# A third slot holds a block of the second chunk's mix; the first twenty gathers go round six slots

## The reference

```python
q = (xc @ w_q).reshape(PEER_CHUNK, PEER_HEADS, 2, PEER_HALF)
sc = jnp.einsum('chid,hikd->chik', q, sub_keys)          # 2 x 128 scores for each head
...                                                       # the best 16 of 16 x 16 sums: 16 experts for each head
u_e = jnp.take(u_tab, expert, axis=0)
v_e = jnp.take(v_tab, expert, axis=0)
act = jax.nn.gelu(jnp.einsum('chkd,cd->chk', u_e, xc))
return jnp.einsum('chk,chkd->cd', gate * act, v_e)
```

## Time and profile before

| | us |
|---|---|
| median of 3 executions | 1703.78 (1702.72 to 1705.15) |
| the profiled execution | 1706.91 |
| its span, first to last instruction | 1704.9 |
| busy in the span: TensorE | 1555.9 (91%) |
| VectorE | 1213.1 (71%) |
| ScalarE | 611.8 (36%) |
| GpSimd | 592.6 (35%) |
| moved by DMA | 675.14 MB, mean 396 GB/s |

### The profile page before, as it was taken

How to read it: one execution, slowest core, us unless ns; L and a number is a source line. 1 busy time by engine, 2 the same in 40 slices (tenths; PEclk the granted TensorE clock), 3 DMA queues, 4 the chain that set the end, 5 groups by cost and what they waited for, 6 DMA issues and landing times.

```text
span 1704.9 us, 19518 instructions
## 1 busy us (share of the span) xinstructions
PE 1555.9 (91%) x6554; PEld 938.1 (55%) x6554; DVE 1213.1 (71%) x3361; ACT 611.8 (36%) x1459; POOL 592.6 (35%) x527
## 2 busy tenths in 40 slices
PE   9999899899999999988998889989999999777776
PEld 8877775447467777544645446535656554232232
DVE  7821899985887659997555677995666777667665
ACT  4142432553344233364332242354433223222222
POOL 0000353442334333343333432343333544443331
PEclk9999999999999999999999999999999999999999
DMA  9655999999999999999999999999999999999996
GB/s 383 254 197 203 372 396 421 404 410 421 421 420 414 416 421 420 420 420 422 421 421 421 421 421 422 388 412 384 421 415 418 421 421 422 421 421 421 422 421 271
DMA packets 93859, 675.14 MB, mean 396 GB/s; under 512 B 10408, under 2 KB 10688, under 8 KB 12224
## 3 DMA queue, kind: packets, MB, share of 16 engines
q0 software_dynamic: 73728, 536.90, 76.2%
q1 hardware_dynamic: 20032, 137.00, 19.8%
HBM read 672.81 MB, written 1.05 MB: 395 GB/s over the span
## 4 chain that ended last, share of the span: by engine, by line
PE 34%; DMA 33%; DVE 13%; ACT 4%; issue 2%; POOL 0%; DVEq 0%; POOLq 0%; ACTq 0%
DMA slots<-expert_rows,expert 33%; PE bank L960 18%; PE bank L466 6%; DVE slots L1961 5%; PE bank L649 3%; PE bank L948 2%; PE bank L945 2%; ACT diag L1460 1%; DVE sg L1499 1%; ACT L1473 1%; DVE htok L1776 1%; DVE coef L1499 1%; DVE x L1499 0%; DVE cands L1942 0%; PE bank L737 0%
## 5 line engine op out<-in xcount | busy, mean ns | idle before, releaser
L960 PE MATMUL bank<-slots,diag 128*128 128x512 f32 x1916 | 907.0, 609 | 127.6 <-ACT diag L1460 123.9
L1088 POOL DMA_INDIRECT slots<-expert_rows,expert x512 | 590.7, 1154 | 1087.3 <-PE bank L960 856.7
L1961 DVE CUSTOM_DVE_ANT_0 slots<-slots,htok 128x1024 f32<-128x1024 f32 x512 | 625.2, 1222 | 266.9 <-DMA slots<-expert_rows,expert 263.0
L960 PEld LDWEIGHTS bank<-slots,diag 128*128 128x128 f32 x1916 | 347.5, 193 | 537.5 <-issue 316.8
L1473 ACT ACTIVATE gel<-dot 128x2 f32<-128x2 f32 (+1 forms) x258 | 52.5, 203 | 597.9 <-DVE dot L1961 589.3
L1460 ACT ACTIVATE diag<-ident,coef 128x128 f32<-128x128 f32 x479 | 168.5, 395 | 204.1 <-DVE coef L1499 195.1
L466 PEld LDWEIGHTS bank<-hT,ring 128*128 128x128 f32 x1488 | 181.6, 194 | 40.9 <-issue 38.4
L466 PE MATMUL bank<-hT,ring 128*128 128x128 f32 x1488 | 182.6, 277 | 1.8 <-DMA ring<-w_blocks 1.0
L1499 DVE SCALAR_TENSOR_TENSOR coef<-gel,ginv,gexp 128x2 f32<-128x2 f32 (+1 forms) x258 | 54.7, 212 | 93.8 <-ACT gel L1473 91.9
L1473 ACT ACT_TABLE_LOAD x67 | 86.0, 1283 | 1.2
L1499 DVE SCALAR_TENSOR_TENSOR sg<-pad,prm,sg 128x128 f32<-128x128 f32 x240 | 71.4, 342 | 0.0
(11 more groups left out here) (353 smaller groups left out, 1544.7 us busy)
## 6 DMA issues: line engine op xcount, KB each, us to landing
ring<-w_blocks SPq DMA_DIRECT2D x90, 1024.0 KB
slots<-w_blocks SPq DMA_DIRECT2D x24, 1024.0 KB, 10.8
slots<-expert_rows,expert POOLq DMA_INDIRECT x512
kept<-w_blocks SPq DMA_DIRECT2D x4, 1024.0 KB, 12.2
keys<-w_blocks SPq DMA_DIRECT2D x2, 1024.0 KB
kv<-w_blocks SPq DMA_DIRECT2D x2, 1024.0 KB, 13.8
prm<-small SPq DMA_DIRECT2D x2, 768.0 KB
x<-x_rows SPq DMA_DIRECT2D x2, 512.0 KB, 11.0
```

Of the source, the lines that this page charges most:

```text
L960: last = mm(bank[h][:, :], diag[:, i % DIAGS, :], slots[:, SLOT[n], D + h * 512:D + (h + 1) * 512], start=m == 0, stop=n == end)
L1088: nc.gpsimd.indirect_dma_start(slots[:, s, :], None, experts_d, bass.IndirectOffsetOnAxis(ap=idx[q % 2][:, k:k + 1], axis=0),).then_inc(ar ...
L1961: v.tensor_tensor_reduce(out=slots[:, s, 0:D], in0=slots[:, s, 0:D], in1=htok[:, ph % 2, :], scale=1.0, scalar=0.0, op0=ALU.mult, op1=ALU.add,
```

## The change

Block 4 of step 1's mix, q1, is held in slot 6 from the opening on, as the third held block, and so it is moved ahead of step 1's other blocks in SP's order and goes no more through the ring. `wq` 3 of step 0, which lay in slot 6, goes to slot 2, where `mo` 0 lay. The first twenty gathers go round six slots (0, 1, 3, 4, 5, 2) instead of seven, and from gather 20 on the gathers go round all nine in another rotation.

```diff
-HELD = {2: 8, 3: 7}
-SLOT = [n % 7 for n in range(20)] + [(6, 8, 0, 1, 7, 2, 3, 4, 5)[n % 9] for n in range(NG - 20)]
+HELD = {2: 8, 3: 7, 4: 6}
+SLOT = [(0, 1, 3, 4, 5, 2)[n % 6] for n in range(20)] + [(0, 1, 3, 8, 4, 7, 5, 6, 2)[n % 9] for n in range(20, NG)]
...
             if ci == 1 and what < 2:
                 return WIDE + STAY + what
+            if ci == 0 and h == 3:
+                return place_of_slot(2)
             if ci == 1 and what in HELD:
                 return place_of_slot(HELD[what])
```

## The result

The changed kernel takes 1708.7 us (median of 17 executions, 1705.89 to 1711.3) against 1703.68 us for the kernel before (17 executions, 1702.72 to 1708.03). The ratio is 1.0026, with a 95% interval of 1.0020 to 1.0033: 4.4 us slower, 3.4 to 5.6 (the two medians are 5.0 us apart). The forecast was 1703.5 us, within 0.2% of no change, and the range ended at 1707.8. It was wrong.

What follows compares the result with a forecast made beforehand. The prediction took DMA's bytes as the bound, with engines late in 228 to 247 us. It summed -2.4 and +2.1 to -0.3 us, forecasting 1703.5 us against the median 1703.78, range 1699.8 to 1707.8.

Steps and rivals of the forecast that it cites:

- What bounds the kernel: Whole kernel: DMA is nearly always full, so bytes moved early count unless it later lacks free slots.
- The new wait in the opening: Opening: `wq` 3 waits for `mo` 0's read; seven loads issue in a row from 155.9 us, none wanted early.
- The load that moves: Opening: q1 goes into idle DMA time, giving a 1.0 MB lead at 186 us, -2.4 us (bounds 0 and -2.5).
- Six slots instead of seven: First twenty gathers: each waits for the add six before; cost +2.1 us, the middle of 0 and +4.1.
- The lead starts the dots earlier: 186 to 228 us: dots wait for DMA, so a lead starts VectorE's full stretch earlier, by up to 2.4 us.
- Gather 25 behind q1's read: Around 247 us: gather 25 cannot go before q1's slot is read, at 246.66 us.
- The fixed round: Rival, gathers of 190 to 233 us: issue-to-data time does not shrink, 3.52 us a gather, 1708.4 us; chance 0.16.
- The lead is kept: Rival, first gathers: a slot's round need take only 16 us, DMA never runs dry, -2.4 us, 1701.4 us; chance 0.20.

Runs made afterwards that it cites:

- wq3_late: Kernel before with only `wq` 3 moved to slot 2, so it and the loads behind it wait for `mo` 0; two held blocks, seven slots: +0.05%.
- before2: The kernel before, unedited, profiled a second time: 1702.80 us.
- eight_slots: Kernel before with one held block instead of two (the gate goes through the ring) and eight slots for the first 24 gathers: +0.15%, 2.6 us slower.
- nine_slots: Kernel before with no held block and nine slots from the first gather: +0.29%, 5.0 us slower.
- six_early: Kernel before with its opening and two held blocks kept, but six slots for the first twenty gathers: +0.35%, 6.0 us slower.
- six_then_seven: Kernel before with six slots for gathers 0 to 11, then seven to gather 19, then nine: +0.12%, 2.0 us slower.
- seven_then_six: Kernel before with seven slots for gathers 0 to 6, then six for gathers 7 to 19, then nine: +0.15%, 2.6 us slower.

## Why the prediction was wrong, point by point

- *What bounds the kernel*: right. DMA's bytes decide, and most of a loss before 250 us is carried to the end.
- *The new wait in the opening*: right, seven loads in a row. The wait costs nothing in wq3_late, where six loads stand in the row.
- *The load that moves, -2.4 us*: the lead was there, and DMA moved 422 GB/s from 158 to 186 us. At 186 us it was 0.9 MB against before2, and 1.7 against the profile from which 1.0 was forecast. That a held block is worth 2.5 us where slots suffice fits eight_slots and nine_slots.
- *Six slots instead of seven, +2.1 us with ends 0 and +4.1*: this step failed. Alone the six slots cost 6.0 us (3.9 to 8.0), about three times the 2.1 that was forecast; the interval just reaches the upper end. The prediction held the issued bytes against the moved ones only at 228 and 237 us, and took DMA for full up to 228 because it was full there before. Its sign, more than 400 GB/s in 206 to 228 us, failed at 381; DMA was short from 198 us on. In the changed kernel's profile the count at 198 us, just behind the longest pause of the gathers, gives 17.8 MB issued and 17.5 moved: all but dry. With the prediction's own figures (11.8 MB by 186 us and 421 GB/s behind it) 16.9 would have been moved and 0.9 left, so that the count at 198 would have warned and not have given the size. It leant besides on 376 GB/s at seven slots as its nearest row, a figure that the second profile does not repeat.
- *The lead starts the dots earlier*: wrong in its sign. Dot 5 came at 201.11 us and dot 11 at 219.01, in before2 at 200.40 and 215.29. That DMA, where slots limit its supply, only comes to its end sooner by being ahead is argued; no run shows it by itself.
- *Gather 25 behind q1's read*: it waited for that read as forecast, at 250.15 instead of some 247, but it is not the cause: six_early, in which q1 is not held, has the whole loss.
- *The fixed round* (chance 0.16, 1708.4 us) comes nearest in time: +7.0 for the slots and -2.4 for the lead, where the runs give +6.0 for the slots and an unsettled part of the lead. In part that is luck, for its mechanism was that the time from issue to data does not shrink, and it does shrink: from issue to dot, gathers 14 to 20 took 11.4 us in the mean in before2, 10.0 in the changed kernel and 8.5 in six_early. It had priced 3.52 us a gather against 3.02; the runs have a smaller difference, 3.06 in six_early and 2.85 in the changed kernel's profile against 2.64 in before2. Its sign, a DMA share below 0.95, came in 206 to 214 us (0.94) and already from 198 (0.90), though not in 214 to 228 (1.01), and over the whole of 206 to 228 the share is 0.98. The split of the loss between six_then_seven (6 gathers that wait for the sixth before them) and seven_then_six (8) fits an even price for each gather, within the error. Of the Trainium skill's rule on gaps and too few buffers ("Perfetto Trace Analysis", section "Optimization Strategy") the prediction said that the trace agrees only in 228 to 247 us; with six slots it agrees from 198 us on.
- *The lead is kept*: its estimate was 16 us for a slot's round with a lone transfer in it, 2.7 us a gather with six slots. From gather 8 to 20 the profiles with six slots have 2.79 to 3.06. The rival overlooked that 2.7 already is too much: a block takes DMA 2.5 us, and from 182.78 to 259.92 us SP issues no weight load beside the gathers in the changed kernel. By the same estimate of 16 us, seven slots make 2.3 us a gather, under the 2.5. That fits a DMA that is full with seven slots and short with six; it is an estimate, worked out from the rows of one gather and one load. The Trainium skill ("DMA: Bandwidth & Descriptors", section "Anatomy of one DMA — SWDGE (gpsimd) path") likewise prices a single DMA, and by its price one gather takes an estimated 4.4 us. With others in the queue it took longer here: in 196 to 240 us a gather landed 8.0 us after its issue in the median in six_early, and 8.8 in before2.

## What to carry to other kernels

Where a buffer is taken from a stream to prefetch something else, count at every pause in the stream's issues, above all at the first one, how many bytes are issued and how many DMA can have moved; bytes that DMA has moved ahead are no longer in that reserve. And hold the time that a buffer's round takes, divided by the number of buffers, against the time that DMA needs for one. A share of 1.01 says that the queue is not empty, not how much is in it: in 186 to 198 us the changed kernel and before2 both show it, and 0.3 and 2.1 MB were left at its end. Here seven buffers kept DMA full and six did not, and nothing shows that two more than seven were worth anything. And one profile is one execution: a shortage in it, of a size with the effect that is argued from it, wants a second profile.

## What the runs showed of the hardware beside this

Two profiles of the same kernel differed by 4.1 us (1706.91 and 1702.80), 1.6 MB of DMA by 320 us. And TensorE's granted clock fell in 186 to 198 us. Waiting for the first dots, TensorE stood idle for 4.25 us before its first add in the changed kernel, for 3.06 in nine_slots, and then had the lower of its two levels (0.50 of full speed, 1.2 GHz) for more than six us: a mean of 0.72 in both. In nine_slots DMA moved 425 GB/s in that stretch and 422 in the next. The lower clock by itself does not make DMA run dry. With six slots it does make the pause longer: the add for which gather 6 waits took 3.78 us in the changed kernel, the next one 1.88. What share of the loss that is stays open; six_early, with a mean of 0.86, loses no less.
